# A hybrid encoder block: TensorE's part of the shift and scale rows from a buffer of its own, between dense matmuls, and ScalarE's order at the border to the down projection

## What is computed

```python
mod = silu(c) @ w_ada + b_ada                       # 2048 -> 6 * 2048
sh1, sc1, gt1, sh2, sc2, gt2 = split(mod, 6)
h = rmsnorm(x, g_norm1) * (1.0 + sc1) + sh1
x = x + gt1 * hybrid_mixer(h, positions, w_in, ..., w_out)   # w_in: 2048 -> 5648
h = rmsnorm(x, g_norm2) * (1.0 + sc2) + sh2
x = x + gt2 * ((silu(h @ w_gate) * (h @ w_up)) @ w_down)     # 5632 wide
return rmsnorm(x, g_final)
```

## Time and profile before

| | us |
|---|---|
| median of three executions | 2417.38 |
| the profiled execution, its time | 2417.64 |
| its span in the trace | 2415.9 |
| TensorE matmuls busy | 2301.4 (95%) |
| VectorE busy | 1522.5 (63%) |
| ScalarE busy | 892.8 (37%) |
| GpSimd busy | 251.2 (10%) |
| DMA | 405.28 MB, mean 168 GB/s |

### The profile page before, as it was taken

How to read it: one execution, slowest core, us unless ns; L and a number is a source line. 1 busy time by engine, 2 the same in 40 slices (tenths; PEclk the granted TensorE clock), 3 DMA queues, 4 the chain that set the end, 5 groups by cost and what they waited for, 6 DMA issues and landing times.

```text
span 2415.9 us, 27445 instructions
## 1 busy us (share of the span) xinstructions
PE 2301.4 (95%) x10500; PEld 1910.0 (79%) x10500; DVE 1522.5 (63%) x1728; ACT 892.8 (37%) x1041; POOL 251.2 (10%) x89
## 2 busy tenths in 40 slices
PE   4898999999998899899999999999999899999997
PEld 4777878888886788788888888888888788888886
DVE  5767565655557556667877787778778534444443
ACT  4232322323235511354444444444444333333332
POOL 0000333333331111100000000000000000000000
PEclk7789989999998999899999999999999999999999
DMA  9843435354453267524434443445444755545452
GB/s 338 299 153 104 159 121 179 112 179 140 153 193 124 76 230 272 189 71 143 163 130 139 156 165 131 132 145 169 134 139 145 283 189 183 200 178 202 178 201 112
DMA packets 188066, 405.28 MB, mean 168 GB/s; under 512 B 9152, under 2 KB 67792, under 8 KB 172368
## 3 DMA queue, kind: packets, MB, share of 16 engines
q1 hardware_dynamic: 174960, 388.01, 45.5%
q10 hardware_dynamic: 13024, 16.13, 1.9%
HBM read 384.19 MB, written 19.92 MB: 167 GB/s over the span
## 4 chain that ended last, share of the span: by engine, by line
PE 80%; DVE 11%; issue 4%; ACT 2%; SPq 1%; DMA 1%; POOL 0%; DVEq 0%; ACTq 0%; POOLq 0%
PE ps L1698 24%; PE ps L1700 24%; PE ps L1699 24%; DVE acc L1051 2%; DVE qk L1254 1%; PE ps L1829 1%; PE ps L1750 1%; DVE acc L1284 1%; PE ps L2100 1%; PE ps L1729 1%; PE ps L1842 1%; PE ps L1840 1%; PE ps L1941 1%; DVE qk L1251 1%; DMA fr<-in_w_ada 1%
## 5 line engine op out<-in xcount | busy, mean ns | idle before, releaser
L886 ACT ACTIVATE whi<-wraw 128x1024 fp32r<-128x1024 f32 x200 | 212.0, 1061 | 261.6 <-PE ps L1700 136.9
L1698 PE MATMUL ps<-h_hi,whi 128*128 128x512 f32 x720 | 290.3, 403 | 13.9 <-DVE h_lo L1080 13.9
L1530 DVE TENSOR_TENSOR wlo<-wraw,whi 128x1024 fp32r<-128x1024 f32 x200 | 240.5, 1219 | 76.9 <-ACT whi L886 76.9
L1699 PE MATMUL ps<-h_lo,whi 128*128 128x512 f32 x720 | 286.0, 397 | 0.0
L1700 PE MATMUL ps<-h_hi,wlo 128*128 128x512 f32 x720 | 285.8, 397 | 0.0
L1698 PE MATMUL ps<-d_hi,whi 128*128 128x512 f32 x704 | 275.4, 391 | 8.3 <-DVE wlo L1644 8.3
L1699 PE MATMUL ps<-d_lo,whi 128*128 128x512 f32 x704 | 274.9, 390 | 0.0
L1700 PE MATMUL ps<-d_hi,wlo 128*128 128x512 f32 x704 | 274.7, 390 | 0.0
L1639 DVE TENSOR_TENSOR d_lo<-d_raw,d_hi 128x2048 fp32r<-128x2048 f32 x44 | 100.8, 2291 | 256.6 <-ACT d_hi L951 256.6
L1698 PE MATMUL ps<-whi,sk_hi 128*128 128x512 f32 x640 | 251.8, 393 | 4.6 <-DVE u2b L1570 4.6
L1700 PE MATMUL ps<-whi,sk_lo 128*128 128x512 f32 x640 | 249.5, 390 | 0.0
(11 more groups left out here) (293 smaller groups left out, 3902.9 us busy)
## 6 DMA issues: line engine op xcount, KB each, us to landing
araw<-in_w_ada SPq DMA_DIRECT2D x64, 1024.0 KB, 5.6
wraw<-in_w_gate SPq DMA_DIRECT2D x88, 512.0 KB, 3.8
wraw<-in_w_up SPq DMA_DIRECT2D x88, 512.0 KB, 4.7
d_raw<-aT_keep SPq DMA_DIRECT2D x44, 1024.0 KB, 4.8
wraw<-in_w_down SPq DMA_DIRECT2D x44, 1024.0 KB, 7.1
wraw<-in_w_in SPq DMA_DIRECT2D x39, 1024.0 KB, 5.3
acc<-in_w_up SPq DMA_DIRECT2D x40, 512.0 KB, 5.5
fr<-in_w_ada SPq DMA_DIRECT2D x32, 512.0 KB, 7.3
```

The lines of the kernel that those rows point to most:

```text
L886: A(EHI[e % 4], src, ACT.Copy).then_inc(uhi_ok, 1)
L1530: V_.tensor_tensor(ELO[e % 4], src, EHI[e % 4].bitcast(F32), ALU.subtract).then_inc(ulo_ok, 1)
L1698: pe.matmul(o, w_hi, m_hi, start=first, stop=False)
L1699: pe.matmul(o, w_hi, m_lo, start=False, stop=False)
```

## The change

- Four tiles `pe_pair0` to `pe_pair3`, each 128 x 512, take pair 7 of a quarter. They lie in the last 512 columns of `wraw0`, `wraw1`, `whi0` and `whi1`, which the front slots (1536 columns wide) don't use. They have a semaphore of their own, `pair_ld`.
- SP's loop runs over 28 pairs (7 a quarter), all for VectorE. After the load of pair 2 of a quarter it waits for `ada_pe` of the quarter before and issues four loads of 256 KB for pair 7, so in quarter 0 these stand ahead of x block 3, pair 3 and the first weight slot. A wait for all four `ada_pe` stands ahead of the first weight load that is 2048 columns wide.
- TensorE does `ada_direct(0)` ahead of `ada_columns(0)`. In quarters 1 to 3 `ada_direct` is cut into its 8 column tiles (two matmuls each), one behind each of the third to tenth triple of the second front slot, ahead of `ada_columns`.
- The counts of `ada_ld` in later stages follow the smaller number of loads.
- ScalarE does `down_hi(1)` ahead of the two `turned` of the last unit.

```diff
+        pe_pair = [at(f"pe_pair{i}", [P, S], F32, w_off + ((i + 1) * SLOT - S) * 4) for i in range(4)]
...
-            for n in range(32):
-                quarter, pair = n // 8, n % 8
+            for n in range(28):
+                quarter, pair = n // 7, n % 7
                 if n < TB:
                     sp.dma_start(xst[n][:], x[0, n * P:(n + 1) * P, :]).then_inc(x_ld[n], 16)
-                if n >= 4 and (n - 4) % 8 == PAIR_PE:
-                    sp.wait_ge(ada_pe, (n - 4) // 8 + 1)
-                elif n >= 4:
-                    sp.wait_ge(ada_acc, 2 * dve_pairs(n - 3))
+                if n >= 4:
+                    sp.wait_ge(ada_acc, 2 * n - 6)
...
                 if pair in (3, 6):
                     front_slot(2 * quarter + (pair == 6))
+                if pair == PE_AT:
+                    if quarter:
+                        sp.wait_ge(ada_pe, quarter)
+                    for k in range(2):
+                        for q in range(2):
+                            sp.dma_start(pe_pair[2 * k + q][:], ada_rows(quarter, PAIR_PE, k)[:, q, :]).then_inc(pair_ld, 16)
+            sp.wait_ge(ada_pe, 4)
             sp.wait_ge(wlo_ok, 7)
...
@@ ScalarE, the down projection @@
                 if d == 1:
                     gate_low(NCH)
                     gate_high(NCH)
+                down_hi(d)
+                if d == 1:
                     turned(NCH, 1, slice(NU * P, NCH * P))
                     turned(NCH, 0, slice(NU * P, NCH * P))
-                down_hi(d)
...
@@ TensorE @@
+            def ada_direct(quarter, j):
+
+                if j == 0:
                     pe.wait_ge(silu_ok, 1)
-                pe.wait_ge(ada_ld[n % 4], 32 * (n // 4) + 32)
...
+                    pe.wait_ge(pair_ld, 64 * quarter + 64)
+                c0 = 32 + 8 * quarter + j
+                for k in range(2):
+                    last = pe.matmul(ps[5][:, c0:c0 + 1], pe_pair[2 * k + j // 4][:, j % 4 * P:(j % 4 + 1) * P],
+                                     csil[:, 2 * PAIR_PE + k:2 * PAIR_PE + k + 1], start=(k == 0), stop=(k == 1))
+                if j == 7:
+                    last.then_inc(ada_pe, 1)
...
+            def front_slot(s, then=None):
...
                         if k == 1 and t in (2, 5):
                             last.then_inc(w_used, 1)
+                        if then is not None and 2 <= 6 * k + t < 10:
+                            ada_direct(then, 6 * k + t - 2)
...
             x_block(3)
+            for j in range(8):
+                ada_direct(0, j)
             ada_columns(0)
-            ada_direct(0)
             for quarter in range(1, 4):
                 front_slot(2 * quarter - 2)
-                front_slot(2 * quarter - 1)
+                front_slot(2 * quarter - 1, quarter)
                 ada_columns(quarter)
-                ada_direct(quarter)
```

More of the change, by code:

```diff
@@ L152, in program @@
         halfpi = tiny[:, 38:39]
+        w_off = top[0]
         wraw = [sb(f"wraw{i}", [P, SLOT]) for i in range(2)]
@@ L245, in program @@
         ada_ld = [sem(f"ada_ld{i}") for i in range(4)]
+        pair_ld = sem("pair_ld")
         ada_pe, ada_acc, ada_sum0, ada_sum, modp_ok, mod_ok = map(
@@ L292, in program @@
         PAIR_PE = 7
+        PE_AT = 2
         ADA0 = 56
-        def dve_pairs(n):
-            return n - (n + 7 - PAIR_PE) // 8
         ROPE = [convin[:, i, 2:2 + S] for i in range(4)] + [sigo[:, i, :] for i in range(2)] + \
@@ L361, in _, with ada_rows @@
             sp.dma_start(stgc[:], c.rearrange("o (a b) -> (o a) b", b=P)).then_inc(c_ld, 16)
-            for n in range(32):
-                quarter, pair = n // 8, n % 8
+            def ada_rows(quarter, pair, k):
+                return w_ada[0, pair * 256 + k * P:pair * 256 + (k + 1) * P, 0:2 * D].rearrange(
+                    "p (q h c) -> p q h c", q=2, h=4)[:, :, quarter, :]
+            for n in range(28):
+                quarter, pair = n // 7, n % 7
                 if n < TB:
                     sp.dma_start(xst[n][:], x[0, n * P:(n + 1) * P, :]).then_inc(x_ld[n], 16)
-                if n >= 4 and (n - 4) % 8 == PAIR_PE:
-                    sp.wait_ge(ada_pe, (n - 4) // 8 + 1)
-                elif n >= 4:
-                    sp.wait_ge(ada_acc, 2 * dve_pairs(n - 3))
+                if n >= 4:
+                    sp.wait_ge(ada_acc, 2 * n - 6)
                 for k in range(2):
                     sp.dma_start(RING[n % 4][:, k * 1024:(k + 1) * 1024].rearrange("p (q c) -> p q c", q=2),
-                                 w_ada[0, pair * 256 + k * P:pair * 256 + (k + 1) * P, 0:2 * D].rearrange(
-                                     "p (q h c) -> p q h c", q=2, h=4)[:, :, quarter, :]).then_inc(ada_ld[n % 4], 16)
+                                 ada_rows(quarter, pair, k)).then_inc(ada_ld[n % 4], 16)
                 if pair in (3, 6):
                     front_slot(2 * quarter + (pair == 6))
+                if pair == PE_AT:
[5 more added lines that the diff above has]
+            sp.wait_ge(ada_pe, 4)
             sp.wait_ge(wlo_ok, 7)
@@ L1049, in ada_pair @@
                     else:
-                        dve.wait_ge(ada_acc, 2 * dve_pairs(n) + k)
+                        dve.wait_ge(ada_acc, 2 * n + k)
                         V_.scalar_tensor_tensor(out=acc[:, half], in0=slot, scalar=csil[:, kt:kt + 1],
@@ L1086, in _ @@
                         mean_square(pair)
-                    ada_pair(8 * quarter + pair)
+                    ada_pair(7 * quarter + pair)
                     if quarter == 0 and pair < TB:
@@ L1300, in body @@
                         if kind == "end":
-                            ada_b(i % 2, 32, i, 8 + i, i == 0, 16 * (16 + 16 + i // 2 + 1))
+                            ada_b(i % 2, 32, i, 8 + i, i == 0, 16 * (14 + 16 + i // 2 + 1))
                         else:
-                            ada_b(i % 2, h * 8 - 8, i, i, i == 0, h * 64 + 16 * (16 - 4 + i // 2 + 1))
+                            ada_b(i % 2, h * 8 - 8, i, i, i == 0, h * 64 + 16 * (14 - 4 + i // 2 + 1))
                     if mixing and j < 4:
@@ L1384, in ada_late @@
             def ada_late(n):
-                ada_b(n % 2, 40, n, 8 + n % 8, n % 8 == 0, 16 * (16 + 20 + n // 2 + 1))
+                ada_b(n % 2, 40, n, 8 + n % 8, n % 8 == 0, 16 * (14 + 20 + n // 2 + 1))
             for u in range(32):
@@ L1739, in ada_columns @@
                 last.then_inc(ada_sum0, 1)
-            def ada_direct(quarter):
-                n = 8 * quarter + PAIR_PE
-                if quarter == 0:
+            def ada_direct(quarter, j):
+                if j == 0:
                     pe.wait_ge(silu_ok, 1)
-                pe.wait_ge(ada_ld[n % 4], 32 * (n // 4) + 32)
[L1747 to L1754, removed]
+                    pe.wait_ge(pair_ld, 64 * quarter + 64)
[6 more added lines that the diff above has]
+            def front_slot(s, then=None):
                 pe.wait_ge(wlo_ok, s + 1)
```

## The result

The changed kernel takes 2386.49 us (median of four, 2385.87 to 2387.11) against 2417.2 us; the ratio is 0.9873 with a 95% interval of 0.9856 to 0.989. The forecast was 2387.1 us, range 2380 to 2395. Run again on another chip it took 2387.46 us against 2416.54 us (0.9883, 0.9867 to 0.99). The profiled execution has a span of 2384.5 us, 31.4 us less than before.

A forecast was written before the change was run, and what follows sets the result against it. Mostly dense TensorE matmuls bound the kernel; gains lay where TensorE does small matmuls alone or idles. 2417.6 - 16.8 (cycles) - 3.0 (quarter 0) - 8.3 - 2.4 (border) = 2387.1 us, range 2380 to 2395.

The forecast's parts named there:

- The direct matmuls between dense ones: Quarters 1 to 3: interleaved direct matmuls cost their own length, 3.46 us a quarter instead of 6.84, slowing no neighbours.
- The columns at full clock: Front stage: columns follow dense work at once, so 16 records take 1.73 us, before 2.54 to 3.57 us.
- The cycle: Front stage, modulation start to modulation start: 27.1 us instead of 32.72, a gain of 16.8 us over three cycles.
- Quarter 0: Start of front stage: modulation at 48.7 us instead of 51.73, gaining 3.0 us despite 2.8 us queue delay.
- The transfers at nothing: Front-stage loads: a quarter's 9.96 MB takes 27.1 us, equal to TensorE's cycle, costing nothing with 3 us in hand.
- The gain passes through whole: After the front stage: everything waits by semaphore on what came before, so the whole front gain carries through.
- The border: Second down weights: TensorE's 8.3 us stall goes, and 12 matmuls at full rate save 2.4 us more.
- The clock: Rival, gaps between dense slots: clock stays up, each restart saves 1.8 us, 5.4 us in three, 2381.7 us; 8%.
- The transfers: Rival, front stage: queue keeps 340 GB/s, a quarter takes 29.3 us, total 2390.7 to 2393.5 us; 15%.
- the border's step 2: Rival, border: weights or VectorE late, or step 2 stalls instead; up to 10.7 us return, 2397.8 us; 6%.
- half clock in the interleaved slots: Rival, front stage: interleaving holds dense slots at half clock, cycle 44.9 us, total 2440 us, slower; 3%.

The follow-up runs named there:

- The run in one piece: Changed kernel with the direct matmuls of quarters 1 to 3 uncut, between the second front slot and the columns; 2393.56 us, ratio 0.9901.
- the kernel with the border alone: Kernel before the change with only ScalarE's new order, down_hi(1) ahead of the two turned; 2406.82 us against 2416.58 us, ratio 0.9959.
- the front part alone: Changed kernel with ScalarE's old order put back at the border; 2401.24 us, ratio 0.9936.
- TensorE's 3.7 us taken out: Changed kernel without the direct matmuls of quarters 1 to 3, their share missing from the rows, loads kept; 2383.41 us.

## Why the prediction was right

*The direct matmuls between dense ones.* Right, and the largest term. They do not leave the path: the chain still goes through those of quarters 1 to 3, as the sum had it, at 3.46 us a quarter forecast and 8 x 0.47 = 3.7 us measured, of which 0.11 us a group is a longer first dense matmul. What they lose is the time at half clock: they took 6.84 us a quarter before. Of the last cycle's 5.3 us (32.72 to 27.44) 3.1 us come from that, 0.85 us from the columns at full clock, and 1.4 us from TensorE's wait for VectorE, which is now filled. The price rested on a misread row: the four records in the earlier trace rows are matmuls with 128 moving columns (the operands are `prT` and `V`), not the same kind with one column:

```profile
792.71 0.60 PE L1941 MATMUL ps<-V,prT 128*128 128x128 f32 x4
```

That their 0.45 us came close to the 0.47 us here is in part luck. The price of the earlier trace rows for one column, 0.108 us a record, was sound: it gives 0.43 us a group.

The Trainium skill's line that a weight load overlaps a running matmul only where row groups differ ("TensorE: Matmul & The Clock Gate", Part 3, The mechanism) would give, as an estimate with one more load of 0.108 us, 0.54 us a group: the measured 0.47 us lies between that and my 0.43.

*The columns at full clock.* 1.73 us forecast, 1.69 measured. The run in one piece shows that this hangs on the interleaving and not on the place before the wait, which I had not priced.

*The cycle.* 27.1 us forecast, 27.75, 27.50 and 27.44 measured, so 15.5 us gained in three cycles where I had 16.8. The missing 0.3 to 0.6 us a cycle are the 0.3 us of the groups and a restart that took 11, 10 and 9 half-clock matmuls where I took nine. VectorE was no longer last, as forecast: its last accumulation ended 2.5 to 2.8 us before the columns started, where I had 2.1. The gain hangs on the trace of the kernel before: the three cycles took 98.2 us there and 96.1 us in the kernel with the border alone, so against the latter it is 13.4 us.

*Quarter 0.* 48.7 us forecast, 47.73 measured: a gain of 4.0 instead of 3.0 us. The queue delayed x block 3 by 2.3 us (27.38 for 25.11 us) instead of 2.8, and pair 4 arrived at 35.06 instead of 35.6 us. The two sides met as forecast, 44.28 us for TensorE and 43.4 for VectorE. The time of this modulation varies by itself: in the other traces with the same quarter 0 it stands at 47.5 to 48.7 us.

*The transfers at nothing.* Right for the changed kernel: VectorE waits for no DMA in quarters 1 to 3 and the queue is full (share 1.05, 380 GB/s on average) from 46 to 88 us. The cover is thin, as forecast: with TensorE's 3.7 us taken out, ScalarE waited 6.0 us for a weight slot and VectorE 1.4 us for a pair. The figure of about 358 GB/s from the Trainium skill ("DMA: Bandwidth & Descriptors", Specifications) did not bind there; 380 GB/s over 42 us lie above it.

*The gain passes through whole.* Right within 3 us only. The stages between the front and the feed-forward part, with the same instructions, took 861.9 to 865.2 us. In the two traces compared this gave 1.0 us more than the parts; with the front part alone it took 1.8 us back.

*The border.* 10.7 us forecast, 10.85 measured, in every kernel with the new order. The next for which ScalarE had to wait was step 3, whose operands landed at 1904.7 and 1908.6 us behind the residual; in the count of the kernel before that is 1925 and 1929 us, where I had 1926. Its low half was ready at 1912.8 us, before TensorE needed it at 1914.9 us.

*The rivals.* The clock did fall in every gap. The transfers, the border's step 2 and half clock in the interleaved slots did not come about. That the sum came within 0.6 us is partly luck: the cycles gave 1.3 us less, quarter 0 and the middle 1.0 us more each, and the same instructions differ by 2 to 3 us from trace to trace, in the front stage of the kernel before and in the middle.

## What to carry to other kernels

Small matmuls that feed a wait were cheapest here cut up between dense ones, ahead of the wait: they cost about their own length at full clock, and the clock of what follows is kept, which a solid piece of them lost. Before pricing a second gain, look at the side that comes next (here VectorE's, which ended 2.5 to 2.8 us before TensorE's, and in quarter 0 less than 1 us before) and at the clock that an engine with less to do will have. At a border between stages, convert the next step's operands before the outputs of the last, if the outputs wait for an engine that is still at work.

## What was not expected of the hardware

3.46 us of one-column matmuls behind dense work, with TensorE never idle, and the granted clock went from 1.00 to 0.50, while the same matmuls mixed with dense triples left it at 1.00. Four fp32 matmuls of 384 columns held 1.00 over a gap of 3.5 us that otherwise ended at 0.50; behind columns that had already run at 0.50 they did not raise it. Behind the same gap the restart took 9 to 11 half-clock matmuls within one execution. With the same instructions the front stage of the kernel before differed by 2.5 us between two traces, mostly by when the clock fell.
